# Where the token sums of a second half stand among the first MLP products, and how its products and its third weight are ordered

## The chip, the cores and the metric

The kernel runs on one core of a Trainium2 chip. The metric is the time of one execution in microseconds (us) on the device. Besides the timed executions there is one profiled execution, from which all rows below are taken. TensorE is called PE (its weight loads PEld), VectorE DVE, ScalarE ACT, GpSimd POOL and SyncE SP.

## The reference, cut to what matters

A trunk of two layers runs over 256 context tokens and 512 latent tokens (768 together) of 1024 features. Around the change each layer computes, from the output `y` of its mixing part and the residual `x`:

```
x  = x + g1 * rms_norm(y, norm_mix_post)
hx = rms_norm(x, norm_mlp_pre) * (1 + sc2) + sh2
x  = x + g2 * rms_norm(square(relu(hx @ w_mlp1)) @ w_mlp2, norm_mlp_post)      # 1024 -> 4096 -> 1024
```

The first layer does this for all 768 tokens, the last for the 512 latent tokens alone.

## The kernel before, in words

All engines run their own hand-written order of work and meet at semaphores. Features lie on the partitions in 8 blocks of 128 (`KB`), tokens along the free dimension. A float32 product is made of three products of rounded parts: high weight with low data, high with high, low with high. So each weight tile is split after its 1 MB load: ACT copies it into a rounded high part (`high_part`, line 1453), and DVE takes the difference in place (`low_part`, line 1887). Loads go through a ring of three slots; SP issues a load (line 599) when PE has made the last product with the slot's old contents. The high parts of the MLP weights alternate between two tiles, `w_high[0]` and `w_high[1]`. The MLP of a layer has 32 such loads, j = 0 to 31, each with two units (output blocks of 128 features), and every unit is 8 blocks of input features times three products.

A norm needs the sum of squares over the features. ACT squares, DVE adds some squares, and PE multiplies the squares by a matrix of ones in plain float32 (`part_sum`, line 817); ACT turns the sum into a root with a logarithm and an exponential (`part_root`, lines 1424 and 1431).

Between the output projection (line 1286) and the MLP the tokens are worked in two parts. In the first layer (`lo == 0`) part 0 is the 256 context tokens and part 1 the 512 latent ones; in the last layer (`lo == 256`) each part has 256 tokens. For each part there are two norms: `norm1` over the projected `y`, with 2 sum products (DVE has added the rest) and `norm2` over the new residual, with 8, one for each block. After `norm2`'s root the chain of the part is, block by block: DVE scales (line 2343), ACT modulates (line 1495), POOL rounds to the high part (line 716), DVE subtracts for the low part (line 2346); each block so finished raises `h_low_ready`, for which PE waits before that block's products (`mlp_start`, line 1320). Only loads j = 0 and 1 are worked by parts; from j = 2 on PE does both parts together (line 1341).

PE's order after the last unit of the output projection is, in both layers:

```
part_sum(l, "norm1", 1, (0, KB - 1))
...
mlp_start(0, 0)
mlp_start(1, 0)
part_sum(l, "norm2", 1, range(KB))
mlp_start(0, 1)
mlp_start(1, 1)
```

`mlp_start(j, p)` does both units of load j for part p. ACT has, in its order: the second part's `take_part`s (lines 1475, 1476), `high_part(l, 1)`, the root of `norm1`, the eight squares of the residual (line 1486), the root of `norm2`, the modulations, and only then `high_part(l, 2)`, which waits until both units of j = 0 are finished, since it writes `w_high[0]`. DVE has `low_part(l, 1)`, the normed additions (`add_normed`, lines 1919 and 1922), `scale_part(1)`, and then `low_part(l, 2)`. After that, for each unit, ACT takes the result from PSUM (line 1827) and DVE squares and splits it (lines 2370 to 2372); `high_part` and `low_part` of load j + 2 follow the two units of load j.

The tile `state` (`S`) is 128 x 2048 and idle in this stage: its last reader is the output projection, which has a high weight part in it.

Of the kernel before, what the change touches and what calls it, by code (L numbers as in the profile page):

```python
# [13 lines left out]
KB = D // 128  # L14
# [33 lines left out]
NSLOT = 3  # L48
# [53 lines left out]
def trunk_program(nc, x, ctx, c, c_ctx, w_ada, b_ada, norm_mix_pre, norm_mix_post, norm_mlp_pre, norm_mlp_post,  # L102
# [4 lines left out]
    ALU, ACT, AX = mybir.AluOpType, mybir.ActivationFunctionType, mybir.AxisListType  # L107
    stack = ExitStack()
    with stack:
# [20 lines left out]
        ring, ring_r = both("weights", [128, NSLOT, 2048])  # L130
# [8 lines left out]
        S, S_r = both("state", [128, 4, 512])  # L139
# [96 lines left out]
        w_high = [R_r[:, :, :].rearrange("p a b -> p (a b)")[:, 16 * TOK + 2048 * i:16 * TOK + 2048 * (i + 1)] for i in range(2)]  # L236
# [26 lines left out]
        def piece(i):  # L263
            return Yf[:, 4 * TOK + 512 * i:4 * TOK + 512 * (i + 1)].rearrange("p (h d) -> p h d", h=H)
        W = [chunks(4)[:, i] for i in range(NC)]
        kend = [piece(4), piece(5)]

        def lhs(ci, d):

# [43 lines left out]
        def each(name):  # L313
# [23 lines left out]
        w_high_ready, w_low_ready, h_low_ready, sum_ready = (  # L337
            sem(n) for n in ("w_high_ready", "w_low_ready", "h_low_ready", "sum_ready"))
# [88 lines left out]
        def mlp_load(j):  # L427

            q, r = divmod(j, 8)
            return ("mlp1", 4 * q + r) if r < 4 else ("mlp2", 4 * q + r - 4)  # L430

        def slot(l, what, i=0):
            return LOADS.index((l, what, i)) % NSLOT
# [286 lines left out]
        def _(pe):  # L720
# [79 lines left out]
            def part_pair(l, what, i, p):  # L800

                if p == 1:
                    return part_of_pair(free_pair(l, what, i), l, p)
                before = UNITS[number(UNITS, 0, what, i) - 4]
                pe.wait_ge(part_evac, len(PARTS_EVAC) * l + PARTS_EVAC.index(before) + 1)
                return part_of_pair(pair(number(UNITS, l, what, i)), l, p)

            def part_sum(l, what, p, blocks_of):

                dst = part_pair(l, what, 0, p)  # L810
                a, b = part_tokens(l, p)
                for k in blocks_of:
                    if what == "norm1" and k == 0:
                        pe.wait_ge(squares_added, 3 * l + p + 1)
                    else:
                        pe.wait_ge(sq_ready, number(SQUARES, l, what, (p, k)) + 1)
                    mm(dst, ones, square_buffer(what, k, 0)[:, a:b], start=(k == 0), stop=(k == KB - 1)).then_inc(sq_used, 1)
# [52 lines left out]
            for l in range(DEPTH):  # L870
# [425 lines left out]
                for u in range(4, 8):  # L1296
# [6 lines left out]
                        out_products(u, dst, [(0, *second)], OUT_BLOCKS).then_inc(gemm_out, 1)  # L1303
                    if u == 5:
                        part_sum(l, "norm2", 0, range(KB))
                part_sum(l, "norm1", 1, (0, KB - 1))

                def mlp_parts(j):
                    pe.wait_ge(w_low_ready, 32 * l + j + 1)
                    return [z.rearrange("p (k n) -> p k n", k=KB) for z in (w_high[j % 2], ring_r[:, slot(l, *mlp_load(j)), :])]  # L1310

                def mlp_start(j, p):
                    high, low = mlp_parts(j)
                    a, b = part_tokens(l, p)
                    dst = [part_pair(l, "mlp1", u, p) for u in (2 * j, 2 * j + 1)]
                    for k in range(KB):
                        pe.wait_ge(h_low_ready, 16 * l + 8 * p + k + 1)
                        for u in range(2):
                            for w, r in ((high, Hm_r), (high, Y_r), (low, Y_r)):
                                last = mm(dst[u], w[:, k, 128 * u:128 * u + 128], r[:, k, a:b],  # L1320
                                          start=(k == 0 and r is Hm_r), stop=(k == KB - 1 and w is low))
                            if k == KB - 1 and p == 1:
                                last.then_inc(gemm_out, 1)
                mlp_start(0, 0)
                mlp_start(1, 0)
                part_sum(l, "norm2", 1, range(KB))
                mlp_start(0, 1)
                mlp_start(1, 1)
                for j in range(2, 32):
                    what, i = mlp_load(j)  # L1330
                    high, low = mlp_parts(j)
# [25 lines left out]
        def _(act):  # L1357
# [89 lines left out]
            def high_part(l, j):  # L1447

                n = LOADS.index((l, *mlp_load(j)))
                act.wait_ge(w_in_s[n % NSLOT], landed(n))  # L1450
                if j >= 2:
                    act.wait_ge(*weights_used(LOADS.index((l, *mlp_load(j - 2)))))
                af(w_high[j % 2], ring[:, n % NSLOT, :], ACT.Copy).then_inc(w_high_ready, 1)  # L1453

            def take_and_square(l, lo):

# [25 lines left out]
            def square_part(l, b, p):  # L1482

                a, e = part_tokens(l, p)
                x_done(act, 3 * l + p, b)
                af(square_buffer("norm2", b, 0)[:, a:e], X[:, b, a:e], ACT.Square).then_inc(sq_ready, 1)
# [33 lines left out]
            for l in range(DEPTH):  # L1520
# [293 lines left out]
                part_root(l, "norm1", 1)  # L1814
                for b in range(KB):
                    square_part(l, b, 1)
                part_root(l, "norm2", 1)
                modulate(l, 2, A2, mods[:, l, 24:32, :])
                for j in range(32):
                    what, i = mlp_load(j)  # L1820
                    if j == 0:
                        high_part(l, 2)
                    for u in (2 * i, 2 * i + 1):
                        src, b = finished(l, what, u), u % 8
                        src = parts_of_pair(src, l) if j < 2 else tokens(src, lo)
                        if what == "mlp1":
                            copied(l, what, u, af(hid[:, b, lo:], src, ACT.Relu, bias=zero_col))  # L1827
                        elif u < 8:
                            copied(l, what, u, af(total[:, b, lo:], src, ACT.Copy))
                        else:  # L1830
                            if u >= 10:
                                act.wait_ge(sum_ready, 24 * l + u - 9)
                            copied(l, what, u, af(partial[:, b % 2, lo:], src, ACT.Copy))  # L1833
                            if u >= 24:
                                act.wait_ge(sum_ready, 24 * l + u - 7)
                                square(l, "norm3", b, Hm[:, b, lo:], lo)
                                act.wait_ge(sq_ready, number(SQUARES, l, "norm3", b) + 1)
                                for a, e, t in segments(lo):
                                    last = af(Hm[:, b, a:e], Hm[:, b, a:e], ACT.Identity, bias=zero_col, scale=G2[:, b, t:t + 1])
                                last.then_inc(scaled, 1)  # L1840
                    if 0 < j < 30:
                        high_part(l, j + 2)
# [7 lines left out]
        def _(dve):  # L1850
# [32 lines left out]
            def low_part(l, j):  # L1883

                at = slot(l, *mlp_load(j))
                dve.wait_ge(w_high_ready, 32 * l + j + 1)
                v.tensor_tensor(ring_r[:, at, :], ring[:, at, :], w_high[j % 2], ALU.subtract).then_inc(w_low_ready, 1)  # L1887

            def proj_low_part(l, s):

# [65 lines left out]
            for l in range(DEPTH):  # L1956
# [398 lines left out]
                    add_square(l, "norm1", b, *second, key=(1, b))  # L2355
                low_part(l, 1)
                add_normed(l, "norm1", *second, 1)
                scale_part(1)
                for j in range(32):
                    what, i = mlp_load(j)  # L2360
                    if j == 0:
                        low_part(l, 2)
                    for u in (2 * i, 2 * i + 1):
                        b = u % 8
                        if what == "mlp2" and u < 8:
                            continue
                        dve.wait_ge(gemm_evac, number(UNITS, l, what, u) + 1)
                        if what == "mlp1":
                            z = hid[:, b, lo:]
                            v.tensor_tensor(hid_high[:, b, lo:], z, z, ALU.mult)  # L2370
                            link(v.tensor_tensor(z, z, z, ALU.mult))
                            v.tensor_tensor(hid_low[:, b, lo:], z, hid_high[:, b, lo:], ALU.subtract).then_inc(hid_ready, 1)
                        else:
                            if u >= 16:
                                dve.wait_ge(sum_ready, 24 * l + u - 15)
                            dst = (Hm if u >= 24 else total)[:, b, lo:]
                            v.tensor_tensor(dst, total[:, b, lo:], partial[:, b % 2, lo:], ALU.add).then_inc(sum_ready, 1)  # L2377
                            if 25 <= u < 31:
                                add_square(l, "norm3", b, lo, TOK)
                    if 0 < j < 30:  # L2380
                        low_part(l, j + 2)
# [43 lines left out]
```

## Time and profile before

| what | us |
|---|---|
| three timed runs | 2481.17, 2485.43, 2493.20 (median 2485.43) |
| the profiled execution, its own time | 2492.08 |
| the span of the profile | 2490.3 |
| PE busy / DVE / ACT / POOL | 2314.6 / 1297.4 / 910.1 / 231.6 |
| first layer, sums of part 1 of `norm2` until the first product of part 1 | from 846.44 to 858.51 |
| last layer, end of the output projection until the first sum of `norm1`, part 1 | from 2100.6 to 2105.15 |
| last layer, idle before the first product of part 1 | 3.29 |
| mean granted PE clock | 0.962 |

The span runs from the first to the last instruction. The profiled execution took 1.8 us more than its span and 6.65 us more than the median of the timed runs. In a row of the timeline a number in square brackets is the idle time of that engine before the row, with what ended it; successive matrix products overlap in their rows, so their rate is read from the distance of their starts. The granted clock is 1.00 for 2.4 GHz and 0.50 for 1.2 GHz.

### The profile page before, as it was taken

The page shows a single profiled execution, that of the slowest core. Times are in us where ns is not written, and L with a number is a line of the kernel's source. Part 1 is how long each engine was busy: PE and PEld are TensorE (multiplying, and loading weights), DVE is VectorE, ACT ScalarE, POOL GpSimd, SP SyncE. Part 2 cuts the span into 40 slices and gives each one's busy share as a digit, 9 for nine tenths or more (in the row PEclk, how much of TensorE's full clock was granted, in tenths as well). Part 3 has the DMA queues.
Part 4 walks back from the last instruction along what each step waited for, and adds up shares of the span by engine and source line. Part 5 has one row for each costly group of instructions (what it writes and reads, how often), then busy time and mean ns, then how long its engine had stood idle before and what let it go on. Part 6 is the DMA issues. An engine that isn't in the chain of part 4 may idle for free.

```text
span 2490.3 us, 37567 instructions
## 1 busy us (share of the span) xinstructions
PE 2314.6 (93%) x16470; PEld 1944.2 (78%) x16470; DVE 1297.4 (52%) x1891; ACT 910.1 (37%) x1322; POOL 231.6 (9%) x204
## 2 busy tenths in 40 slices
PE   7999999987989999999999799999994989999997
PEld 5889797875758788888888588878783768888885
DVE  4689652248363641424234669955238465533454
ACT  5373423224364422212213537342322455322223
POOL 3044200000030100000000103400000020000000
PEclk9999999997999999999999899989996999999998
DMA  8213401234211122212212221430222212232331
GB/s 301 60 52 112 143 1 51 68 101 135 79 35 35 34 68 68 68 51 68 68 51 68 85 70 42 136 119 18 68 68 65 79 35 69 85 100 86 102 102 51
DMA packets 159274, 192.83 MB, mean 77 GB/s; under 512 B 18134, under 2 KB 129208, under 8 KB 158599
## 3 DMA queue, kind: packets, MB, share of 16 engines
q1 hardware_dynamic: 154864, 183.63, 22.5%
q10 hardware_dynamic: 3543, 6.43, 0.8%
q8 instruction: 130, 2.13, 0.3%
q0 software_dynamic: 704, 0.37, 0.2%
q14 instruction: 33, 0.27, 0.0%
HBM read 181.98 MB, written 8.44 MB: 76 GB/s over the span
## 4 chain that ended last, share of the span: by engine, by line
PE 85%; DVE 7%; ACT 4%; issue 2%; DMA 1%; POOL 0%; DVEq 0%; SPq 0%; ACTq 0%
PE ps L1341 34%; PE ps L755 19%; PE ps L1286 4%; PE ps L785 2%; PE ps L1320 2%; PE ps L973 2%; PE ps L1232 2%; PE ps L844 2%; PE ps L979 2%; PE ps L1087 1%; DVE region L2218 1%; PE ps L742 1%; PE ps L1260 1%; PE ps L1245 1%; DVE residual L2104 1%
## 5 line engine op out<-in xcount | busy, mean ns | idle before, releaser
L1341 PE MATMUL ps<-region_r 128*128 128x512 f32 (+1 forms) x1536 | 379.3, 356 | 0.0
L1341 PEld LDWEIGHTS ps<-region_r 128*128 128x128 f32 x1536 | 270.4, 188 | 42.8
L1341 PE MATMUL ps<-region_r,weights_r 128*128 128x512 f32 (+1 forms) x768 | 232.2, 357 | 0.0
L1887 DVE TENSOR_TENSOR weights_r<-weights,region_r 128x2048 fp32r<-128x2048 f32 x64 | 146.5, 2288 | 129.8 <-ACT region_r L1453 129.8
L1341 PE MATMUL ps<-mixed_r,region_r 128*128 128x512 f32 (+1 forms) x672 | 203.7, 358 | 0.0
L1341 PE MATMUL ps<-mixed_r,weights_r 128*128 128x512 f32 (+1 forms) x672 | 203.2, 357 | 0.0
L1341 PE MATMUL ps<-modulated_r,region_r 128*128 128x512 f32 (+1 forms) x672 | 201.0, 354 | 0.0
L1341 PEld LDWEIGHTS ps<-region_r,weights_r 128*128 128x128 f32 x768 | 144.6, 188 | 23.2
L1827 ACT ACTIVATE region<-ps,cst 128x768 f32<-128x768 f32 (+1 forms) x64 | 50.5, 795 | 303.8 <-PE ps L1341 294.8
L755 PE MATMUL ps<-residual_r,weights_r 128*128 128x256 f32 (+1 forms) x576 | 160.8, 347 | 0.0
L2370 DVE TENSOR_TENSOR region_r<-region 128x768 fp32r<-128x768 f32 (+1 forms) x64 | 52.7, 824 | 192.2 <-ACT region L1827 192.2
L1341 PEld LDWEIGHTS ps<-mixed_r,weights_r 128*128 128x128 f32 x672 | 126.5, 188 | 20.4
L1341 PEld LDWEIGHTS ps<-modulated_r,region_r 128*128 128x128 f32 x672 | 126.6, 188 | 19.1
L1341 PEld LDWEIGHTS ps<-mixed_r,region_r 128*128 128x128 f32 x672 | 126.2, 188 | 18.2
L1453 ACT ACTIVATE region_r<-weights 128x2048 fp32r<-128x2048 f32 x64 | 122.2, 1909 | 12.6 <-PE ps L1320 8.1
L755 PEld LDWEIGHTS ps<-residual_r,weights_r 128*128 128x128 f32 x576 | 108.1, 188 | 14.9 <-issue 0.5
L1833 ACT ACTIVATE region<-ps 128x768 f32<-128x768 f32 (+1 forms) x48 | 33.8, 705 | 219.6 <-PE ps L1341 219.6
L755 PE MATMUL ps<-region_r,state_r 128*128 128x256 f32 (+1 forms) x360 | 90.5, 356 | 15.5 <-DVE region_r L1899 12.6
L755 PE MATMUL ps<-region_r,weights_r 128*128 128x512 f32 (+1 forms) x384 | 104.3, 347 | 0.0
L2377 DVE TENSOR_TENSOR region<-region 128x768 f32<-128x768 f32 (+1 forms) x32 | 26.4, 826 | 141.5 <-ACT region L1833 141.5
L1894 DVE TENSOR_TENSOR weights_r<-weights,state_r 128x2048 fp32r<-128x2048 f32 x18 | 41.2, 2291 | 111.5 <-ACT state_r L1439 111.5
L755 PEld LDWEIGHTS ps<-region_r,state_r 128*128 128x128 f32 x360 | 66.0, 195 | 29.2 <-issue 16.6
(382 smaller groups left out, 4988.5 us busy)
## 6 DMA issues: line engine op xcount, KB each, us to landing
weights<-in_w_mlp SPq DMA_DIRECT2D x64, 1024.0 KB, 5.4
weights<-in_w_ada SPq DMA_DIRECT2D x40, 1024.0 KB, 5.2
weights<-in_w_in SPq DMA_DIRECT2D x34, 1024.0 KB, 5.2
region<-in_w_ada SPq DMA_DIRECT2D x8, 1024.0 KB, 17.0
weights<-in_w_out SPq DMA_DIRECT2D x8, 1024.0 KB, 6.7
x_kept<-residual SPq DMA_DIRECT2D x2, 3072.0 KB, 12.3
region<-decays_kept ACTq DMA_DIRECT2D x4, 1536.0 KB, 10.6
residual<-x_kept SPq DMA_DIRECT2D x2, 3072.0 KB, 10.1
```

The costliest lines, as they stand in the source:

```text
L755: last = mm(dst[:, CTX + a:CTX + b], w[:, k, m], r[k][:, a:b], start=(k == 0 and w is high and r is r_high), stop=(k == KB - 1 and r is r_ ...
L785: last = mm(dst[:, CTX + a:CTX + b], mat, sq[:, a:b], start=(k == 0), stop=(k == n - 1))
L844: last = mm(ps[32 * k:32 * k + 32, bank, :], cs[:, 4 * half + k, :], w[:, k, :], start=(half == 0), stop=(half == 1))
L973: last = mm(ps[:, ci, 128 * h:128 * h + 128], NT[:, ci, h, :], inverse_alternate(ci, size, h), start=True, stop=True)
L979: last = mm(ps[:, ci, 128 * h:128 * h + 128], W[ci][:, h, :], TT_alternate(ci, size, h), start=True, stop=True)
L1232: last = mm(dst[:, CTX + s0:CTX + s1], QH[0:96, h, 128 * qt:128 * qt + 128], KH[0:96, h, s0:s1], start=True, stop=True)
L1286: last = mm(dst[:, at:at + b - a], w[:, k, m], r[:, a:b], start=(k == 0 and part_of == "low"), stop=(k == 5 and w is low))
L1341: last = mm(dst[:, CTX + a:CTX + b], w[:, k, m], r[:, a:b], start=(k == 0 and r is r_low), stop=(k == KB - 1 and w is low))
L1453: af(w_high[j % 2], ring[:, n % NSLOT, :], ACT.Copy).then_inc(w_high_ready, 1)
L1827: copied(l, what, u, af(hid[:, b, lo:], src, ACT.Relu, bias=zero_col))
L1887: v.tensor_tensor(ring_r[:, at, :], ring[:, at, :], w_high[j % 2], ALU.subtract).then_inc(w_low_ready, 1)
L2370: v.tensor_tensor(hid_high[:, b, lo:], z, z, ALU.mult)
```

## The change

PE: in the first layer the sum of `norm1`, part 1, stays where it was; `norm2`'s eight sum products of part 1 are split, three ahead of the first two blocks of load 1's products of part 0, five behind these two blocks and ahead of the other six. In the last layer the sum of `norm1`, part 1, goes behind load 0's products of part 0, and `norm2`'s sum stays behind load 1's. In both layers the products of part 1 for loads 0 and 1 run in one loop over the blocks: for each block four units instead of two. ACT and DVE: load 2 is split into the `state` tile, ahead of the root of `norm2`, part 1, on ACT, and ahead of `scale_part(1)` on DVE; it no longer waits for load 0's units. All other loads keep their tiles.

```diff
+        def mlp_high(j):
+
+            return S_r[:, :, :].rearrange("p a b -> p (a b)") if j == 2 else w_high[j % 2]
...
-                part_sum(l, "norm1", 1, (0, KB - 1))
+                if lo == 0:
+                    part_sum(l, "norm1", 1, (0, KB - 1))
...
-                def mlp_start(j, p):
-                    high, low = mlp_parts(j)
+                def mlp_start(loads, p, ks=range(KB)):
+                    weights = [mlp_parts(j) for j in loads]
                     a, b = part_tokens(l, p)
-                    dst = [part_pair(l, "mlp1", u, p) for u in (2 * j, 2 * j + 1)]
-                    for k in range(KB):
+                    dst = [part_pair(l, "mlp1", u, p) for j in loads for u in (2 * j, 2 * j + 1)]
+                    for k in ks:
                         pe.wait_ge(h_low_ready, 16 * l + 8 * p + k + 1)
-                        for u in range(2):
+                        for n, o in enumerate(dst):
+                            high, low = weights[n // 2]
+                            m = slice(128 * (n % 2), 128 * (n % 2) + 128)
                             for w, r in ((high, Hm_r), (high, Y_r), (low, Y_r)):
-                                last = mm(dst[u], w[:, k, 128 * u:128 * u + 128], r[:, k, a:b],
+                                last = mm(o, w[:, k, m], r[:, k, a:b],
                                           start=(k == 0 and r is Hm_r), stop=(k == KB - 1 and w is low))
                             if k == KB - 1 and p == 1:
                                 last.then_inc(gemm_out, 1)
-                mlp_start(0, 0)
-                mlp_start(1, 0)
-                part_sum(l, "norm2", 1, range(KB))
-                mlp_start(0, 1)
-                mlp_start(1, 1)
+                mlp_start([0], 0)
+                if lo:
+                    part_sum(l, "norm1", 1, (0, KB - 1))
+                    mlp_start([1], 0)
+                    part_sum(l, "norm2", 1, range(KB))
+                else:
+                    part_sum(l, "norm2", 1, range(3))
+                    mlp_start([1], 0, range(2))
+                    part_sum(l, "norm2", 1, range(3, KB))
+                    mlp_start([1], 0, range(2, KB))
+                mlp_start([0, 1], 1)
...
-                if j >= 2:
+                if j >= 3:
                     act.wait_ge(*weights_used(LOADS.index((l, *mlp_load(j - 2)))))
-                af(w_high[j % 2], ring[:, n % NSLOT, :], ACT.Copy).then_inc(w_high_ready, 1)
+                af(mlp_high(j), ring[:, n % NSLOT, :], ACT.Copy).then_inc(w_high_ready, 1)
...
+                high_part(l, 2)
                 part_root(l, "norm2", 1)
                 modulate(l, 2, A2, mods[:, l, 24:32, :])
                 for j in range(32):
                     what, i = mlp_load(j)
-                    if j == 0:
-                        high_part(l, 2)
...
                 add_normed(l, "norm1", *second, 1)
+                low_part(l, 2)
                 scale_part(1)
                 for j in range(32):
                     what, i = mlp_load(j)
-                    if j == 0:
-                        low_part(l, 2)
```

## Rows read from the trace of the kernel before

**Rows 1.** The page: busy time by engine, and the chain of waits by engine.

```profile
PE 2314.6 (93%) x16470; PEld 1944.2 (78%) x16470; DVE 1297.4 (52%) x1891; ACT 910.1 (37%) x1322; POOL 231.6 (9%) x204
...
PE 85%; DVE 7%; ACT 4%; issue 2%; DMA 1%; POOL 0%; DVEq 0%; SPq 0%; ACTq 0%
```

**Rows 2.** Chain of waits, first layer; start us, length us, what.

```profile
822.02 10.89 PE ps L1286 x48
...
834.93 11.51 PE ps L1320 x96
...
846.44 6.88 PE ps L817 x16
...
854.89 0.70 DVE modulated L2343
...
858.51 24.12 PE ps L1320 x96
```

**Rows 3.** Timeline of ACT, both layers; start us, length us, instruction.

```profile
834.10 1.91 ACT L1453 ACTIVATE region_r<-weights 128x2048 fp32r<-128x2048 f32 x1
...
840.18 0.64 ACT L1486 ACTIVATE region<-residual 128x512 f32<-128x512 f32 x1 [2.83 <-DVE residual L1922]
...
847.40 1.23 ACT L1486 ACTIVATE region<-residual 128x512 f32<-128x512 f32 x2 [0.57 <-DVE residual L1922]
...
2113.43 0.75 ACT L1486 ACTIVATE region<-residual 128x256 f32<-128x256 f32 x2 [0.25 <-DVE residual L1922]
```

**Rows 4.** Timeline of PE, last layer.

```profile
2100.46 0.28 PE L1286 MATMUL ps<-region_r,weights_r 128*128 128x256 f32 x1
...
2105.15 1.78 PE L817 MATMUL ps<-region,k_f_sb 128*128 128x256 f32 x4 [4.41 <-DVE region L1872]
```

**Rows 5.** Chain of waits, last layer.

```profile
2086.30 0.86 PE ps L817 x4
...
2097.71 0.43 DVE modulated_r L2346
...
2106.93 12.41 PE ps L1320 x96
...
2119.34 3.47 PE ps L817 x16
...
2126.08 13.17 PE ps L1320 x96
...
2139.25 20.88 PE ps L1341 x92
```

**Rows 6.** Timeline of DVE, last layer.

```profile
2103.33 0.42 DVE L2346 TENSOR_TENSOR modulated_r<-modulated,mixed_r 128x256 fp32r<-128x256 f32 x1 [0.30 <-POOL mixed_r L716]
...
2123.95 1.10 DVE L2343 TENSOR_TENSOR modulated<-residual,region 128x256 f32<-128x256 f32 x3 [10.21 <-ACT region L1431]
...
2137.74 0.68 DVE L2370 TENSOR_TENSOR region_r<-region 128x512 fp32r<-128x512 f32 x1
...
2145.46 2.28 DVE L1887 TENSOR_TENSOR weights_r<-weights,region_r 128x2048 fp32r<-128x2048 f32 x1
```

**Rows 7.** Windows: length, busy of five engines, granted clock, DMA share, GB/s.

```profile
858.50:861.00 2.50, 2.49 (x6) 2.02 (x7) 2.50 (x4) 1.20 (x2) 1.05 (x2) 0.50 0.00 0
...
1952.80:1954.50 1.70, 0.05 (x2) 0.00 (x1) 1.24 (x6) 0.74 (x2) 0.48 (x1) 1.00 0.00 0
...
1954.50:1956.50 2.00, 1.97 (x6) 1.04 (x7) 0.00 (x0) 1.97 (x3) 0.56 (x2) 1.00 0.24 70
...
2126.08:2129.30 3.22, 3.22 (x15) 3.22 (x16) 3.22 (x8) 1.99 (x4) 1.92 (x5) 0.50 0.00 0
...
880.00:1290.00 410.00, 410.00 (x2320) 355.54 (x2319) 140.35 (x117) 85.58 (x74) 0.00 (x0) 1.00 0.19 62
```

**Rows 8.** Landing times of all MLP loads, and of two together (1609 us).

```profile
DMA to landing us min/median/max: 5.0/5.4/6.5
...
DMA to landing us min/median/max: 5.1/6.3/7.4
```

More of the change, by code:

```diff
@@ L1305, in _ @@
                         part_sum(l, "norm2", 0, range(KB))
-                part_sum(l, "norm1", 1, (0, KB - 1))
+                if lo == 0:
+                    part_sum(l, "norm1", 1, (0, KB - 1))
                 def mlp_parts(j):
                     pe.wait_ge(w_low_ready, 32 * l + j + 1)
-                    return [z.rearrange("p (k n) -> p k n", k=KB) for z in (w_high[j % 2], ring_r[:, slot(l, *mlp_load(j)), :])]
-                def mlp_start(j, p):
-                    high, low = mlp_parts(j)
+                    return [z.rearrange("p (k n) -> p k n", k=KB) for z in (mlp_high(j), ring_r[:, slot(l, *mlp_load(j)), :])]
+                def mlp_start(loads, p, ks=range(KB)):
+                    weights = [mlp_parts(j) for j in loads]
                     a, b = part_tokens(l, p)
-                    dst = [part_pair(l, "mlp1", u, p) for u in (2 * j, 2 * j + 1)]
-                    for k in range(KB):
+                    dst = [part_pair(l, "mlp1", u, p) for j in loads for u in (2 * j, 2 * j + 1)]
+                    for k in ks:
                         pe.wait_ge(h_low_ready, 16 * l + 8 * p + k + 1)
-                        for u in range(2):
+                        for n, o in enumerate(dst):
+                            high, low = weights[n // 2]
+                            m = slice(128 * (n % 2), 128 * (n % 2) + 128)
                             for w, r in ((high, Hm_r), (high, Y_r), (low, Y_r)):
-                                last = mm(dst[u], w[:, k, 128 * u:128 * u + 128], r[:, k, a:b],
+                                last = mm(o, w[:, k, m], r[:, k, a:b],
                                           start=(k == 0 and r is Hm_r), stop=(k == KB - 1 and w is low))
@@ L1886, in low_part @@
                 dve.wait_ge(w_high_ready, 32 * l + j + 1)
-                v.tensor_tensor(ring_r[:, at, :], ring[:, at, :], w_high[j % 2], ALU.subtract).then_inc(w_low_ready, 1)
+                v.tensor_tensor(ring_r[:, at, :], ring[:, at, :], mlp_high(j), ALU.subtract).then_inc(w_low_ready, 1)
             def proj_low_part(l, s):
```

## The prediction

> **What bounds the kernel now.** I read the page first, then the chain of waits around the two places that the diff touches, then the timelines of the engines there, then windows for the clock. PE is busy 93% of the span and holds 85% of the chain that ended last [rows 1], so only PE's idle time and its slow time are to be had. In the long MLP stretch from 880 to 1290 us PE is busy for all 410.00 us at clock 1.00 [rows 7]: what ends earlier ahead of it ends the layer earlier by as much, and what is late inside it costs in full. The idle time lies ahead of it. In the first layer the sums of norm2, part 1, end at 846.44 + 6.88 = 853.32, and the first product of part 1 starts at 858.51 [rows 2]; between them are root, scaling, modulation, rounding and difference of one block. In the last layer the projection's last product starts at 2100.46, and PE waits 4.41 us for DVE's added squares before the sum of norm1 at 2105.15 [rows 4]; after norm2's sums (2119.34 + 3.47 = 2122.81) it waits again until 2126.08 [rows 5]. After each wait PE comes back at 1.2 GHz: the clock is 0.50 in 858.50 to 861.00 and in 2126.08 to 2129.30 [rows 7].
>
> What one product costs at full clock: 10.89 / 48 = 0.227 us with 512 tokens, 11.51 / 96 = 0.120 us with 256 [rows 2]. A sum product costs 6.88 / 8 = 0.86 us with 512 tokens [rows 2] and 3.47 / 8 = 0.43 us with 256 [rows 5]. So the slow clock cost 24.12 - 96 x 0.227 = 2.3 us in the first layer, and 13.17 - 96 x 0.120 = 1.65 us in the last [rows 2, 5]. The number of products and sums is the same before and after; only their order changes.
>
> **First layer.** Until the end of load 0's products of part 0, nothing changes: 834.93 + 48 x 0.120 = 840.7. Now come three sums. Their squares end at 840.18 + 0.64 = 840.82 and then every (847.40 - 840.18) / 6 = 1.20 us [rows 3], so PE waits about 0.3 us twice and has the three at 844.1. Two blocks of load 1 are 12 products, 1.4 us, and 0.2 for the change of kind: 845.7. Five sums, 4.3 us: 850.0 (the last square ends at 847.40 + 1.23 = 848.6, in time). The sums are ready 3.3 us earlier than before, and 36 products, 4.3 us, cover what follows: PE is busy until 854.4. The order of ACT and DVE takes part of this back. ACT's split of load 2 now stands between the squares and the root: 848.6 + 1.8 = 850.45 (1.81 us from 834.10 to the next start, [rows 3]); DVE's takes 2.2 to 2.3 us (2.28, [rows 6]): 852.7. The root alone would let DVE scale at 850.45 + (854.89 - 853.32) = 852.0, so the split ends last there and costs 0.7 us. From the start of scaling to PE's first product there are 858.51 - 854.89 = 3.62 us [rows 2]: PE starts at 856.3 instead of 858.5, a gain of 2.2 us.
>
> PE's wait shrinks from 5.2 to 1.9 us. What a wait of this length does to the clock this kernel shows elsewhere: PE idles for 1.70 us from 1952.80 and the clock is 1.00 there and behind it [rows 7]. I take it that the clock holds: the 96 products cost 96 x 0.227 + 0.2 = 22.0 us instead of 24.1, a gain of 2.1. If it falls after all, the gain is nothing. They don't starve: a block is now 12 products, 2.7 us, while in the last layer the next block was there every (2103.33 - 2097.71) / 7 = 0.80 us [rows 5, 6], or 1.6 with twice the tokens (an estimate). First layer together: 4.3 us.
>
> **Last layer.** The first part's blocks are there when the projection ends: the first difference ends at 2097.71 + 0.43 = 2098.1 [rows 5], the eighth at 2103.33 + 0.42 = 2103.75 [rows 6]. PE starts at 2100.6 and takes 6 x 0.12 = 0.72 us for a block, so it comes to the eighth at 2105.6 and waits for none: 4.4 us of idle time goes, and with it the slow clock behind it (12.41 - 11.5 = 0.9 us in the products, 1.78 - 0.86 = 0.9 us in the sums, [rows 4, 5]). What is late next: load 0's products end at 2106.4, the two sums of norm1 (0.86, [rows 5]) at 2107.3, some 0.4 us later than before (2106.93), and ACT's residual squares, which ended at 2113.43 + 0.75 = 2114.2 [rows 3], end by 2114.6. Load 1's products end at 2113.0 and norm2's sums, 3.5 us, at 2116.5. ACT's split ends at 2116.3, DVE's at 2118.5; the root alone would be there at 2116.5 + (2123.95 - 2122.81) = 2117.6, so the split costs 0.9 us. Scaling starts at 2118.5, and PE's products (2126.08 - 2123.95) = 2.1 us later [rows 5, 6], at 2120.6. PE waits 4.1 us instead of 3.3, and I leave the 96 products at their measured 13.17 us: 2133.8 instead of 2139.25, a gain of 5.5 us. The slow clock behind this wait is bounded by the two rows: nothing to 2.3 us, against the 1.65 that stand in it.
>
> **Edits that I cost at nothing.** Load 2's copy no longer waits for load 0's units. It needs its load landed: SP issues it when the projection ends (2100.6), and MLP loads take 5.0 to 6.5 us [rows 8], so it is there by 2107, with ACT at 2114.6; without this cover ACT and with it the root would be late. The four units of loads 0 and 1 now end with the last block together. PE needs the first of their four PSUM pairs at once for load 2; in the last block unit 0 ends three units, 9 x 0.12 = 1.1 us, ahead of the end, and ACT's copy takes about 0.7, so it is just covered; uncovered it costs up to 0.7 us. Load 3 is issued only when unit 1 is finished, at the end of this stretch (call it T), and not half-way. It lands at T + 5, and ACT's split ends at T + 7. DVE has four units to square and split first, (2145.46 - 2137.74) = 7.7 us [rows 6], then load 3's split, 2.3: T + 10.0. PE has load 2's 48 products, 10.9 us, until then. A margin of 0.9 us in the last layer, and over 4 us in the first. Load 4 is issued right behind load 3; two loads issued together landed after 5.1 and 7.4 us [rows 8], so the first of two isn't held up.
>
> **The sum.** 4.3 + 5.5 = 9.8 us. The profiled execution took 2492.08 us (span 2490.3): it would take 2482.3. It lies 6.7 us above the median of the timed runs; against the median of 2485.43 the forecast is 2475.7, call it 2476.
>
> **The rivals.**
> *The clock falls in the first layer too* (2476 + 2.3 = 2478). For it: both waits of 3.3 us and more were followed by 0.50 [rows 7], and the stretch now has three waits, two of 0.3 and one of 1.9. Against it: the 1.70 us row. Chance 0.15.
> *Load 3 is late in the last layer.* If DVE or the load takes 1 us longer than my margin, PE waits in the midst of the products. The price is at least the lateness, at most that of a load of 7.4 us instead of 5.1 (2.3 less the slack that ACT has before DVE, so about 2) and one more slow start, 2.3: 2478 to 2480. For it: a margin of under 1 us. Against it: the loads of the MLP took 6.5 us at most. Chance 0.12.
> *Slower than before: PE stays at 1.2 GHz in the new loop over four units.* Its place is the 2 x 96 products of part 1, which now go round four PSUM regions instead of two, and the stretch of short waits and sums in front. At half clock a product cost 2.50 / 6 = 0.42 us with 512 tokens and 3.22 / 15 = 0.21 with 256 [rows 7]: 96 x 0.19 + 96 x 0.09 = 27 us of slow time against the 4 paid now, so 2476 + 23 + 2 = 2501. It decides against the change when more than 10 us beyond today's are lost, that is when over a third of these products run slow on top. For it: only that PE comes out of its waits slow. Against it: with two units in the loop the slow time ended while products ran, after a cost of 2.3 and 1.65 us, and the 410 us at 1.00, in which PE goes round all four PSUM pairs. Chance 0.06.
>
> Against these 410 us stands a rule of the Trainium skill (TensorE: Matmul & The Clock Gate, A second HAM failure mode: psum-queue depth-cycling): a kernel that cycled through PSUM banks between its groups of products went to and fro between the two clock levels. By it the last rival's 2501 would be the forecast; the trace disagrees, since units change pairs all through rows 7's 410 us at 1.00.
>
> **The chances.** My own case has 0.67, the others 0.15, 0.12 and 0.06. Bounds that move it: the clock in the first layer (0 to 2.1 of gain), the slow start in the last (0.7 worse to 1.65 better), load 3 (up to 4 worse). The gain is then 3 to 11.5 us, which is 2474 to 2482; the three timed runs lie 12 us apart, so a median of a few runs is good for 4 to 6 us: 2467 to 2487. A measurement of this kernel can tell about 0.5%, 12.4 us, from no change; my 9.8 us is 0.39%. So most of my own case falls within 0.5%, a third of it beyond by the spread of the medians: faster 0.24, same 0.69, slower 0.07.
>
> **What would show it.** In the profile after: in the last layer no idle ahead of norm1's sum, products at 0.12 us from the projection's end on, and about 4 us of wait ahead of the 96 products; in the first layer a wait of some 2 us in place of 5.2 with the clock at 1.00 behind it and 22 us for the 96 products; DVE's split of load 2 as the last thing before scaling in both; no wait of PE between load 2 and load 3. I am wrong if PE waits at load 2 or 3, if the splits end after the root by more than 1 us, or if the clock is 0.50 after the first layer's wait.

## The result, and the profile after

The changed kernel took 2467.07 us (median of nine runs, 2461.88 to 2475.80); the kernel before 2490.91 us (median of nine, 2481.17 to 2493.20). The ratio estimated from all runs is 0.9924, 95% interval 0.9909 to 0.9939, that is some 19 us less (15 to 23). The two medians by themselves lie 23.8 us apart and the two means 20.2, so by how much the change is faster is known to a few us only. The forecast was 9.8 us less, to 2476, with a range of 2467 to 2487. The profiled execution took 2475.80 us, its span is 2474.0 us, 16.3 less than before. Line numbers are 4 to 13 higher than before.

From the page of the changed kernel, span, busy time and chain by engine:

```profile
span 2474.0 us, 37566 instructions
...
PE 2302.1 (93%) x16470; PEld 1938.7 (78%) x16470; DVE 1299.5 (53%) x1891; ACT 910.7 (37%) x1322; POOL 233.4 (9%) x204
...
PE 84%; DVE 8%; ACT 4%; issue 3%; DMA 1%; POOL 0%; DVEq 0%; SPq 0%; ACTq 0%
```

The chain of waits of the changed kernel, first layer (start, length, what); it answers to [rows 2]:

```profile
821.69 10.90 PE ps L1290 x48
...
847.07 0.63 ACT region L1499
...
848.21 1.90 ACT state_r L1466
...
850.14 1.36 DVE weights_r L1899
...
852.35 0.70 DVE modulated L2355
...
855.96 22.01 PE ps L1327 x96
877.96 12.21 PE ps L1354 x70
```

The last square (847.07) is followed by ACT's split of load 2 into `state`, DVE's, and then at once by scaling (852.35): the split ends last, as forecast. The 96 products take 22.01 us instead of 24.12. The timeline of PE has the wait ahead of them (in brackets), to be read against the 5.2 us between 853.3 and 858.5 of before ([5.19] in the same view of the kernel before):

```profile
855.96 0.47 PE L1327 MATMUL ps<-modulated_r,region_r 128*128 128x512 f32 x1 [1.87 <-DVE modulated_r L2358]
```

The same view, last layer, against [rows 5]:

```profile
2092.25 1.81 ACT region_r L1466
...
2094.08 2.30 DVE weights_r L1899
...
2096.43 6.01 PE ps L1327 x48
2102.44 3.47 PE ps L821 x16
...
2109.18 13.23 PE ps L1327 x96
2122.41 37.62 PE ps L1354 x165
```

The timeline of PE there, two waits in brackets. The 4.41 us of [rows 4] are gone, but the first wait below is new, 1.06 us for DVE's split of load 1, and the second, ahead of part 1, is 3.28 us:

```profile
2096.43 0.38 PE L1327 MATMUL ps<-modulated_r,region_r 128*128 128x256 f32 x1 [1.06 <-DVE weights_r L1899]
...
2109.18 0.35 PE L1327 MATMUL ps<-modulated_r,region_r 128*128 128x256 f32 x1 [3.28 <-DVE modulated_r L2358]
```

DVE's timeline of the last layer shows that the split of load 2, forecast as the last thing before scaling, ended earlier here; scaling waited 0.57 us longer, for the root:

```profile
2104.19 2.29 DVE L1899 TENSOR_TENSOR weights_r<-weights,state_r 128x2048 fp32r<-128x2048 f32 x1 [2.28 <-ACT state_r L1466]
2107.05 1.09 DVE L2355 TENSOR_TENSOR modulated<-residual,region 128x256 f32<-128x256 f32 x3 [0.57 <-ACT region L1444]
```

That is the expected part, and it holds 9.2 us: from the projection's last product to load 2's first it was 49.9 us in the first layer and is 45.6, and it was 38.6 in the last and is 33.8. Most of the rest stands where nobody waits for anything, in the first layer's long MLP stretch. Windows of the changed kernel (length, busy of PE, PEld, DVE, ACT, POOL, each with its number of instructions, clock, DMA):

```profile
855.96:877.96 22.00, 22.00 (x98) 18.25 (x99) 10.38 (x14) 6.09 (x8) 4.90 (x8) 1.00 0.03 3
885.00:1365.00 480.00, 480.00 (x2771) 423.15 (x2770) 171.75 (x144) 113.17 (x104) 0.00 (x0) 1.00 0.20 64
```

and the same 480 us of the kernel before:

```profile
885.00:1365.00 480.00, 480.00 (x2719) 416.31 (x2718) 167.79 (x140) 107.69 (x97) 0.00 (x0) 1.00 0.20 63
```

PE is busy throughout and at clock 1.00 in both, but it makes 2771 products instead of 2719. A product of 256 tokens and one of 512 stand in turn here; a pair takes 480 / (2719 / 2) = 353.1 ns before and 346.4 after (353.3 and 346.7 from the starts themselves, over the whole stretch). The groups by shape (window 900 to 1370, mean ns in the last column but one) say which of the two it is; first after, then before:

```profile
L1354 PE MATMUL ps<-region_r 128*128 128x512 f32 x499 | 184.0, 391 | 0.0
...
L1354 PE MATMUL ps<-region_r 128*128 128x256 f32 x499 | 139.7, 280 | 0.0
```

```profile
L1341 PE MATMUL ps<-region_r 128*128 128x512 f32 x472 | 177.7, 399 | 0.0
...
L1341 PE MATMUL ps<-region_r 128*128 128x256 f32 x472 | 131.8, 279 | 0.0
```

The 512-wide product drops from 399 to 391 ns; the 256-wide one stays (279 and 280). The ends of products are modelled in these rows, but the starts say the same: behind a 512-wide product the next one starts after 236.7 ns before and 230.0 after, behind a 256-wide one after 116.7 in both. For 30 loads of 48 pairs that is 1440 x 6.6 ns = 9.5 us, as much as the whole of what was forecast.

### The profile page after: what moved, and what is told of

It is laid out like the page before. It is cut to its first block, busy times and chain, and to the rows that moved or that the text cites. A ratio compares the mean times of both kernels' runs of the same rounds, so it can differ in the third digit from the quotient of the medians.

```text
span 2474.0 us, 37566 instructions
## 1 busy us (share of the span) xinstructions
PE 2302.1 (93%) x16470; PEld 1938.7 (78%) x16470; DVE 1299.5 (53%) x1891; ACT 910.7 (37%) x1322; POOL 233.4 (9%) x204
## 4 chain that ended last, share of the span: by engine, by line
PE 84%; DVE 8%; ACT 4%; issue 3%; DMA 1%; POOL 0%; DVEq 0%; SPq 0%; ACTq 0%
PE ps L1354 33%; PE ps L759 19%; PE ps L1290 4%; PE ps L789 3%; PE ps L977 2%; PE ps L1236 2%; PE ps L983 2%; PE ps L848 2%; PE ps L1327 2%; PE ps L1091 1%; DVE region L2230 1%; PE ps L746 1%; PE ps L1264 1%; PE ps L1249 1%; DVE residual L2116 1%
## 5 line engine op out<-in xcount | busy, mean ns | idle before, releaser
L1354 PE MATMUL ps<-modulated_r,region_r 128*128 128x256 f32 (+1 forms) x624 | 186.6, 353 | 0.0
L1354 PE MATMUL ps<-mixed_r,region_r 128*128 128x256 f32 (+1 forms) x624 | 186.5, 353 | 0.0
L1354 PEld LDWEIGHTS ps<-modulated_r,region_r 128*128 128x128 f32 x624 | 117.2, 188 | 16.7
L1354 PEld LDWEIGHTS ps<-mixed_r,region_r 128*128 128x128 f32 x624 | 117.2, 188 | 16.7
L1845 ACT ACTIVATE region<-ps 128x768 f32<-128x768 f32 (+1 forms) x48 | 33.8, 705 | 215.8 <-PE ps L1354 215.8
```

Source lines behind the costliest of these rows:

```text
L1354: last = mm(dst[:, CTX + a:CTX + b], w[:, k, m], r[:, a:b], start=(k == 0 and r is r_low), stop=(k == KB - 1 and w is low))
```

## The experiments

All traces are cut at the same places: until the output projection's last product of the first layer (A), from there to load 2's first product (B, the changed stretch), loads 2 to 31 (C), from there to the last layer's last product of the output projection (D), from there to load 2's first product (E, the changed stretch), and the rest (F), in us. Each row is one trace; after and after_again are two traces of the same kernel. A and D hold work that no kernel here changes, and yet they differ from trace to trace by up to 10.6 and 13 us, which is what makes single times so uneven. In the traces with 346.7 ns, load 2 itself, whose high part stands in `state`, has 348.8.

| kernel | A | B | C | D | E | F | ns for a pair in C |
|---|---|---|---|---|---|---|---|
| before | 832.5 | 49.9 | 508.8 | 709.2 | 38.6 | 351.2 | 353.3 |
| after | 832.2 | 45.6 | 499.3 | 711.3 | 33.8 | 351.7 | 346.7 |
| sums_only | 833.0 | 46.0 | 508.8 | 716.3 | 34.1 | 351.5 | 353.3 |
| loop_only | 834.4 | 53.1 | 510.4 | 704.3 | 42.5 | 353.3 | 353.3 from load 3 on |
| split_only | 823.8 | 49.9 | 499.3 | 708.7 | 38.5 | 351.3 | 346.7 |
| after_again | 829.3 | 47.2 | 499.3 | 703.5 | 34.9 | 351.7 | 346.7 |
| state_late | 829.2 | 50.2 | 499.3 | 705.8 | 38.3 | 351.3 | 346.7 |
| state_at_10 | 828.3 | 50.2 | 501.9 | 706.7 | 38.3 | 351.3 | 353.3, then 346.7 |
| shifted | 832.5 | 49.7 | 508.8 | 709.0 | 38.6 | 351.1 | 353.3 |
| split_behind | 827.4 | 44.7 | 499.3 | 710.7 | 33.8 | 351.7 | 346.7 |
| region_far | 831.0 | 49.4 | 508.8 | 705.6 | 38.4 | 351.1 | 353.3 |
| state_even | 828.8 | 50.1 | 500.8 | 710.6 | 38.6 | 354.0 | 348.8 and 346.7 in turn |

**PE's order of the sums alone.** Both layers' sums where the change has them, the products of part 1 load by load, load 2 split late:

```diff
-                part_sum(l, "norm1", 1, (0, KB - 1))
+                if lo == 0:
+                    part_sum(l, "norm1", 1, (0, KB - 1))
...
-                mlp_start(0, 0)
-                mlp_start(1, 0)
-                part_sum(l, "norm2", 1, range(KB))
-                mlp_start(0, 1)
-                mlp_start(1, 1)
+                mlp_start([0], 0)
+                if lo:
...
+                else:
+                    part_sum(l, "norm2", 1, range(3))
+                    mlp_start([1], 0, range(2))
+                    part_sum(l, "norm2", 1, range(3, KB))
+                    mlp_start([1], 0, range(2, KB))
+                mlp_start([0], 1)
+                mlp_start([1], 1)
```

> The change's order of PE's sums alone; the products of part 1 run load by load as before, and load 2 is split late into its old tile. Local terms: first layer, the sums end near 850.0, no split stands ahead of the root, PE starts part 1 2.9 us earlier and at full clock (2.1 more): 5.0. Last layer: 4.4 us of idle goes, part 1 starts 6.3 us earlier. Together 11 us less than before, all of it ahead of the long MLP stretches. The two traces showed something that none of these terms holds: in the first layer's long MLP stretch a pair of products of 256 and 512 tokens takes 353.3 ns before and 346.7 ns after, 9.5 us over 1438 pairs. Theory C (the slow pace is entered because the clock fell and rose ahead of it): the clock stays up in the first layer here, so 346.7 ns, 20 us less than before. Theory T (the tile `state` for load 2 sets the pace): 353.3 ns, 11 us less. Theory R (it falls either way from run to run): no relation.

Measured: 2487.03 us against 2490.61, ratio 0.9974 (0.9951 to 0.9997), 1 to 12 us less. B is 4.0 and E 4.5 us shorter in the trace, 8.5 together where 11 were expected. Its chain in the first layer:

```profile
855.79 8.07 PE ps L1323 x30
...
863.86 15.25 PE ps L1323 x66
879.12 10.95 PE ps L1351 x62
```

Thirty products at 0.27 us and not 0.227, at clock 1.00: load by load a block is used up in 6 x 0.227 = 1.4 us, quicker than it comes, and the 96 products take 23.3 us. In the loop over four units they take 22.0: that is what the loop gives, 1.3 us. And the long stretch stays slow, though the granted clock was 1.00 from 706 us to the end of the stretch, which is against theory C:

```profile
885.00:1365.00 480.00, 480.00 (x2719) 416.35 (x2718) 166.08 (x137) 108.63 (x98) 0.00 (x0) 1.00 0.19 62
```

**The loop over four units alone.**

```diff
-                mlp_start(0, 0)
-                mlp_start(1, 0)
+                mlp_start([0], 0)
+                mlp_start([1], 0)
                 part_sum(l, "norm2", 1, range(KB))
-                mlp_start(0, 1)
-                mlp_start(1, 1)
+                mlp_start([0, 1], 1)
```

> The loop over four units alone, with the sums and load 2's split as before. Load 2's copy waits for load 0's second unit, which is now finished only in the last block: copy 1.9 us, split 2.3 us, so PE waits some 3.5 us ahead of load 2 in each layer, and may come back slow (up to 2 us each): 7 to 11 us more than before. Theory C: the clock falls ahead of part 1 as before, and again ahead of load 2, so 353.3 ns and nothing back. Theory T: 353.3 ns as well. Theory R: no relation.

Measured: 2498.64 us against 2490.61, ratio 1.0032 (1.0003 to 1.0060): 1 to 15 us slower. B and E are longer by 3.1 and 3.8 us, and load 2 starts at half clock in both layers, which adds 1.6 us in C and 2.1 in F: 10.6 us, at the upper end of the 7 to 11 expected. The chain in the last layer shows the wait that the change avoids:

```profile
2127.81 12.47 PE ps L1322 x90
...
2140.37 1.92 ACT region_r L1454
...
2142.32 2.30 DVE weights_r L1888
...
2144.66 20.50 PE ps L1342 x82
```

PE ends the 96 products at 2140.3 and starts load 2 at 2144.66, behind ACT's copy, which had waited for load 0's unit, and DVE's split. So in the change the early split takes away no wait of the kernel before; it takes away the one that the loop would make.

**The early split into `state` alone.** ACT's and DVE's lines of the change, PE's order as before:

```diff
+            return S_r[:, :, :].rearrange("p a b -> p (a b)") if j == 2 else w_high[j % 2]
...
+                high_part(l, 2)
                 part_root(l, "norm2", 1)
...
                 add_normed(l, "norm1", *second, 1)
+                low_part(l, 2)
                 scale_part(1)
```

> The early split of load 2 into `state` alone, with PE's order as before. ACT and DVE are idle behind the squares until PE's sums end (4.7 us in the first layer), so the split is hidden there and load 2 was never waited for: 0 us in the local terms. Theory T: 346.7 ns in the first layer's MLP stretch and so 9.5 us less than before. Theory C: 353.3 ns and no change. Theory R: no relation.

Measured: 2476.56 us against 2490.61, ratio 0.9946 (0.9925 to 0.9967). B and E as before (49.9, 38.5), C 9.5 us shorter. The first window below is the slow clock behind PE's wait, the second the fast pace that follows all the same:

```profile
849.83:852.80 2.97, 2.97 (x7) 2.39 (x8) 2.97 (x4) 1.63 (x2) 1.10 (x2) 0.50 0.00 0
885.00:1365.00 480.00, 480.00 (x2771) 423.22 (x2770) 165.03 (x138) 112.35 (x104) 0.00 (x0) 1.00 0.20 64
```

Together with sums_only this settles theory C: the slow pace doesn't come from the clock.

**The change once more.**

> The changed kernel once more. Theories C and T: 346.7 ns again and 19 us less than before. Theory R: it may be 353.3 ns in this trace.

Measured: 2466.10 us against 2490.61, ratio 0.9902 (0.9876 to 0.9927), and 346.7 ns again. In this trace PE's wait ahead of part 1, 1.87 us as in the other, did end in a slow stretch:

```profile
850.90:853.08 2.18, 0.31 (x3) 0.13 (x2) 1.67 (x3) 1.52 (x3) 1.93 (x3) 1.00 0.00 0
853.08:857.00 3.92, 3.92 (x10) 3.10 (x11) 3.92 (x5) 1.63 (x2) 1.72 (x3) 0.56 0.00 0
```

B is 47.2 us here, against 45.6 in the other trace of the same kernel. So the rival "the clock falls in the first layer too" happens in one execution and not in another, at a price of 1.6 us (23.63 us for the 96 products, not 22.01). The last layer differs too: with the same wait of 3.28 us ahead of part 1 the clock was 0.50 for 6.8 us here and for 3.4 there, and the 96 products took 14.38 us, not 13.23, so E is 34.9 us. B and E are together 9.2 us shorter than before in one trace of the change and 6.4 in the other.

**The tile of load 2 alone.** The kernel before with one edit; the split keeps its late place and its wait:

```diff
+        def mlp_high(j):
+
+            return S_r[:, :, :].rearrange("p a b -> p (a b)") if j == 2 else w_high[j % 2]
```

(and `mlp_high(j)` wherever `w_high[j % 2]` was).

> The kernel before with one edit: the high part of load 2 stands in `state`; when it is split, and what that waits for, stays as it was, and so does PE's order. Local terms: 0. Theory T (the tile of load 2 sets the pace of all loads behind it): in the first layer 348.8 ns for a pair during load 2, as in the three traces with the tile, 346.7 ns for loads 3 to 31, and 9.5 us less than before. Theory E (it is the early split, and so the engines' timing, that sets it): 353.3 ns and no change.

Measured: 2477.19 us against 2489.62, ratio 0.9950 (0.9928 to 0.9973), with B and E as before. The window, to be held against the 2719 products of before:

```profile
885.00:1365.00 480.00, 480.00 (x2771) 423.17 (x2770) 168.38 (x141) 111.85 (x103) 0.00 (x0) 1.00 0.20 63
```

48 pairs out of 1440 read their high weight from another tile, and the other 1392 go faster too. Theory E is refuted: the split is as late as before.

**The same tile for load 10.** `if j == 10` in place of `if j == 2`.

> As state_late, but load 10's high part stands in `state` instead of load 2's. If the tile sets the pace of what follows, one trace holds both: 353.3 ns for loads 2 to 9, some 349 for load 10, 346.7 for loads 11 to 31, that is 21 x 48 x 6.6 ns = 6.7 us less. If it is what happens at the start of the stretch that counts: 353.3 ns for all loads but 10.

Measured: 2478.62 us (one run), 353.3 ns for each of loads 2 to 9, 348.8 for load 10, 346.7 for each of loads 11 to 31, and C 6.9 us shorter. Windows ahead of load 10 and behind it, 5.68 and 5.78 products in a us:

```profile
880.00:1010.00 130.00, 130.00 (x738) 112.72 (x737) 41.94 (x34) 27.00 (x23) 0.00 (x0) 1.00 0.20 65
1035.00:1365.00 330.00, 330.00 (x1906) 290.97 (x1905) 119.08 (x100) 79.21 (x74) 0.00 (x0) 1.00 0.19 62
```

**Both high tiles moved by 1 KB, no `state`.**

```diff
-[:, 16 * TOK + 2048 * i:16 * TOK + 2048 * (i + 1)] for i in range(2)]
+[:, 16 * TOK + 256 + 2048 * i:16 * TOK + 256 + 2048 * (i + 1)] for i in range(2)]
```

> The kernel before with both high tiles of the MLP weights moved by 1 KB within the same region, `state` unused. Theory T-address (a pace belongs to an address): another pace than 353.3 ns. Theory T-history (the pace is kept until a load with another one comes between): 353.3 ns as before.

Measured: 2491.59 us (one run), all loads at 353.3 ns. The same window again holds 2719:

```profile
885.00:1365.00 480.00, 480.00 (x2719) 416.27 (x2718) 167.79 (x140) 107.42 (x97) 0.00 (x0) 1.00 0.20 63
```

**Load 2 in another part of `region`.** As state_late with `R_r[:, 6, 0:2048]` for load 2.

> As state_late, but load 2's high part stands in an idle part of `region`, 8 KB behind the two high tiles, instead of in `state`. If any third tile for one load sets the fast pace: 346.7 ns for loads 3 to 31. If it has to be `state` (or a place like it): 353.3 ns for all.

Measured: 2486.13 us (one run), 353.3 ns for all 30 loads, load 2 too. A third tile as such does nothing. Whether it has to be `state` itself or another place would do as well isn't known: this is the only other place that was tried.

```profile
885.00:1365.00 480.00, 480.00 (x2719) 416.18 (x2718) 166.75 (x139) 108.00 (x97) 0.00 (x0) 1.00 0.19 62
```

**Every even load in `state`.** `if j % 2 == 0 and j >= 2`.

> As state_late, but every even load from 2 on has its high part in `state`. By history (348.8 ns with the tile `state`, 346.7 for any load of `region` once a load of `state` has come before): 348.8 and 346.7 ns in turn, 347.8 in the mean, a stretch of 1440 x 0.3478 = 501 us. If the fast pace needed a long undisturbed stretch of `region`, the odd loads would be at 353.3 ns.

Measured: 2484.77 us (one run), 348.8 and 346.7 ns in strict turn, C 500.8 us. History decides for `region` loads: 346.7 ns once a `state` load has come before in the stretch. In the last layer (F), where all products are 512 wide, this kernel loses 2.8 us.

```profile
885.00:1365.00 480.00, 480.00 (x2763) 421.67 (x2762) 167.84 (x139) 110.91 (x101) 0.00 (x0) 1.00 0.19 62
```

**Load 2's split behind the modulations.** The change with ACT's and DVE's split of load 2 moved back:

```diff
-                high_part(l, 2)
                 part_root(l, "norm2", 1)
                 modulate(l, 2, A2, mods[:, l, 24:32, :])
+                high_part(l, 2)
...
-                low_part(l, 2)
                 scale_part(1)
+                low_part(l, 2)
```

> The changed kernel with load 2's split behind the modulations on ACT and behind scale_part(1) on DVE; tile and PE's order as in the change. By the traces the split costs 0.7 us in the first layer and 0.9 in the last, and PE needs the load only 13 to 22 us later. Expected: PE's wait ahead of part 1 1.2 us (first) and 3.3 us (last) instead of 1.9 and 4.1, 1.6 us less than the changed kernel, so some 20.5 us less than before, with 346.7 ns for a pair. If the split was hidden, no difference between the two.

Measured: 2469.42 us against 2489.62, ratio 0.9927 (0.9893 to 0.9960); the times don't tell it from the change, the traces do. B is 44.7 us, 0.95 less than in the change's trace with the clock up, with a wait of 0.91 us ahead of part 1 in place of 1.87; E is the same 33.8, with the same 3.28 us of wait, against the expected gain of 0.9. The chain in the first layer, root and scaling now one behind the other:

```profile
845.72 0.73 ACT region L1444
...
846.55 0.70 DVE modulated L2355
...
850.17 22.01 PE ps L1327 x96
```

This is the kernel that I would keep, for the 0.95 us in the trace; that it beats the change in time isn't shown.

## Why the prediction was right and wrong

**The first layer** was right in its terms: forecast 4.3 us, measured 4.3 (B) in the first trace. The split of load 2 ends at scaling's start; the wait shrank from 5.2 to 1.87 us (forecast 1.9); the clock held and the 96 products took 22.01 us (forecast 22.0). The doubt about the clock was right too: in after_again it fell, and B was 2.7 us shorter than before. So 4.3 is what this layer gives when the clock holds, and whether it holds is not settled by the 1.70 us row that I relied on. And split_behind confirms the 0.7 us put down to the split, with 0.95.

**The last layer** was near in sum and wrong in one step. Forecast 5.5 us, measured 4.8 (E), and 3.7 in after_again. The step that failed is "Load 1's products end at 2113.0", that is, straight behind the sums of norm1: I checked that the squares, the roots and the first part's blocks were there, and not load 1's own split, which `mlp_start([1], 0)` waits for. ACT's copy of load 1 stands behind two `take_part`s, DVE's split follows it at once (2092.25 and 2094.08 in the chain), and PE waited 1.06 us for it; in sums_only the same split is on the chain (2109.72 to 2112.02 there). My 0.9 us for load 2's split in the last layer then was nothing, since the sums came later than the split: split_behind, without it in the way, has the same E. Two errors of about 1 us, in opposite directions: that the sum came near is in part luck. The slow start there, bounded by me at 2.3 us, cost 14.38 - 96 x 0.120 = 2.9 us in after_again.

**Load 3** was there in time in both layers: no wait of PE stands between load 2 and the end of the MLP in the traces of the change. **The slower rival** is refuted: the 96 products of the loop over four units took 22.01 us, at full clock, in the first layer, and where they started slow (23.63 us in after_again) the clock was back at 1.00 after 3.4 us. The rule named with it (the Trainium skill, TensorE: Matmul & The Clock Gate, A second HAM failure mode: psum-queue depth-cycling) tells of a kernel in which PE was idle for short times between its groups of products. This trace has four PSUM regions in turn without such idle time, PE busy for 22.00 of 22.00 us at clock 1.00 in the window above, so cycling through the regions alone does not bring the clock down here.

**The sum** was about half of what was measured, for a term that it did not have. The step that failed is the first one, "In the long MLP stretch from 880 to 1290 us PE is busy for all 410.00 us at clock 1.00": the rows show that, but I read it as a stretch of fixed length. Busy and at full clock was not the same as at the best pace: `state` for load 2 took it from 353.3 to 346.7 ns for a pair. I had costed the change of tile at nothing but the wait that it removes. Undone and done alone this term shows cleanly: with it in split_only, state_late and split_behind C is 499.3 us, without it in sums_only, shifted and region_far 508.8, and state_at_10 turns it on in the middle of a trace. 9.2 from B and E and 9.5 from C, less the 0.6 that F is longer, are 18.1 us, against 2490.91 x (1 - 0.9924) = 18.9 by the ratio. The trace of after_again has 6.4 in place of 9.2. The 23.8 us between the medians aren't explained by these terms; the rest is of the size by which A and D differ.

**The range** held by luck. 2467.07 lies at its very edge, and the gain lies outside the 3 to 11.5 us that I gave as its bounds. The range reached that far down only because 2474 to 2482 was widened to 2467 to 2487 for the spread of medians, and because the median of the three runs that I started from, 2485.43, was 5.5 us below the median of nine. From 2490.91 the same 9.8 us give 2481.1, 14 us above what was measured. For a gain of more than 0.5% I had a chance of 0.24; it was 0.76% (0.61 to 0.91) by the ratio.

What stays open is why. It isn't the clock (1.00 in all), not the time of the split (state_late), not a third tile (region_far), not a shift of the pair of tiles by 1 KB (shifted), not a slow clock at the start of the stretch (loop_only has one during load 2 and 353.3 ns from load 3 on), and it isn't a property of the `region` loads themselves, since loads 11 to 31 of state_at_10 use the same tiles, slots and PSUM pairs as in the kernel before. What is left is the history of the stretch: a load from `state` changes the pace of what follows, and nothing in the stretch changes it back. It is not chance from run to run either, as far as twelve traces can tell: all seven with a `state` load in the stretch have 346.7 ns behind it, all five without have 353.3. What it is in PE or in the memory that remembers was not isolated, and no place for the tile outside `region` other than `state` was tried, nor another place within `state`. A `state` load in the output projection (its units 4 and 5), ahead of the MLP, does not bring the fast pace.

## What to carry to other kernels

Ask of a stretch that is "100% busy at full clock" how long one product takes there, and compare with the same shape elsewhere in the trace: 353 against 347 ns was to be seen in the kernel before, too: the starts of the output projection's second to fourth unit (769 to 794 us) give 346.7 for a pair of the same widths. When PE's order is changed, list for each moved group every semaphore that it waits for, the weights' own among them; the one left out was the one that ended last. Parts of a change that look independent may not be: the loop alone made the kernel slower, the early split alone removed no wait, and together they work.

## What the runs showed of the hardware

- Products of 256 and 512 columns in turn on one set of weights each have more than one steady pace at one clock: 346.7 and 353.3 ns for a pair, each the mean of every load of 48 pairs for as long as the stretch lasted (353.3 in all 30 loads of before, 346.7 in loads 3 to 31 of after), set by what ran before. With the high weight in `state` a pair takes 348.8 ns.
- In the slow pace the gaps repeat every six products (113, 233, 117, 241, 120, 236 ns from start to start at 1000 us in the trace of before), in the fast one they hardly vary (116 to 117 and 230 ns).
- In stretches of 512 columns alone the tile has a small price: with every even load in `state` the rest of the program from load 2 of the last layer on (F) took 354.0 us instead of 351.2; products start every 230 ns during a load from `state` and every 227 during one from `region`.
- The same wait of PE, 1.87 us in both traces of the changed kernel, left the clock at 1.00 in one and was followed by 3.4 us at 0.50 in the other.
